# mLSTM value products of a two-layer hybrid block: one fp32 product replaced by three products of rounded parts, with the causal masks moved

## The chip, the core and the metric

One core of a Trainium2 chip runs the whole program. The metric is the device time of one execution in microseconds (us). PE is the matrix engine, DVE the vector engine, ACT the scalar engine, POOL the GpSimd engine and SP the queue that issues the weight loads.

## The reference

Two layers of a block over 512 tokens, 256 of context and 256 latent. Each layer projects the normed tokens to the inputs of three branches, merges them, and ends with an MLP. The change touches the mLSTM branch alone: four heads, keys and queries of width 128, values of width 256, each head scanned left to right and right to left.

```
def step(carry, inp):                       # one direction, one chunk
    d = where(tri, bcum[..., :, None] - bcum[..., None, :] + ic[..., None, :], -inf)
    m_t = maximum(inter, max(d, axis=-1))
    w_intra = exp(d - m_t[..., None])
    s_qk = einsum('bhtd,bhsd->bhts', qc, kc) * w_intra
    num = einsum('bhts,bhsv->bhtv', s_qk, vc) + w_inter[..., None] * einsum('bhtd,bhdv->bhtv', qc, c_mat)
    den = sum(s_qk, axis=-1) + w_inter * einsum('bhtd,bhd->bht', qc, n_vec)
    h_out = num / maximum(abs(den), exp(-m_t))[..., None]
...
h = h * rsqrt(mean(h * h, axis=-1) + EPS);  y = h.reshape(..., M_V) * gain * sigmoid(o_pre)
```

The kernel computes it without chunks: for each head and direction one weight matrix over all pairs of tokens (an exponential times the product of key and query), and the value product of it. Context tokens see only context; layer 1 needs the latent outputs alone.

## The kernel before

Tokens come in four tiles of 128 (`TT` = 4): tiles 0 and 1 are context, 2 and 3 latent. The order of all work is written out once, as a list of steps that `make_plan` builds (lines 184 to 443); each engine's program walks the same list and takes from each step what is its own. So an engine does its share strictly in the order of the steps, and waits at semaphores.

Large products (a "panel", 256 output columns by 8 k-tiles of 128) multiply in three products of parts. ACT rounds the weights of a panel to `wH` (L1526), DVE subtracts to get `wL` (L1989), both two panels ahead, and PE runs wH by hH, wL by hH and wH by hL (L1213, L1214, L1217). The parts have the type fp32r.

The steps of one mLSTM head h in layer 0 are, in order:

- `weigh`: PE makes the exponents, m0 and m1, one bank of PSUM for each direction (L1379), and the key-query products of key tiles 0 and 1 (L1386). ACT takes nine exponentials of them into `EP` (L1777, 2,560 columns; first all of one direction, then of the other; eight and 1,792 columns in layer 1).
- `part mo 0:2`: PE runs two of the eight k-tiles of the head's output-gate panel.
- `weigh_late`: PE makes the key-query products of key tiles 2 and 3 (L1394). They go to bank 0, which held m0, so this waits until the last exponential of that direction has read it. DVE then multiplies the exponentials by the products, in place (L2341), after all exponentials are there, and gives `P_ready`; POOL clears the wrong side of the diagonal blocks (L1944) after that.
- `norm_h` of head h-1: ACT squares the last tile of `hM` into `junk` for its sum (L1788), loads the table of the square root and takes it (L1792); DVE takes the reciprocal (L2376) and scales `hM` in place (L2378).
- `part mo 2:6`: four more k-tiles.
- `turn` of head h-1: PE transposes `hM` (L1420); ACT copies to `y_tmp` (L1799), DVE multiplies by the gate `sig_o` (L2387), ACT and POOL split the result (L1536, L1872).
- `value`: PE multiplies `EP` by the values `vaug` (L1410), which have a column of ones behind their 256, so that the denominator comes as column 257. The tiles come in the order 2, 3, 0, 1, each with two banks, one for each direction: 7, 7, 3 and 3 products. Tiles 0 and 1 use the banks of 2 and 3 again. For each tile DVE makes the divisors (L2357, L2361, L2364) and writes `hM` (L2365, L2368); ACT squares the first three tiles (L1788).
- `panel mo`: the last two k-tiles. ACT then splits the weights of a later panel (two L1526) and takes the gate's sigmoid `sig_o` by an exponential (L1592), with a table load ahead of it when the square root's table is in.

Layer 1 has the same steps with two tiles (14 value products a head), and `mo` is one whole panel between `norm_h` and `turn`. Head 0's `weigh` comes earlier there, ahead of the last values panel.

## Time and profile before

| | us |
|---|---|
| median of three runs (1830.58 to 1833.92) | 1832.34 |
| the profiled execution | 1831.94 |
| its span, first to last instruction | 1830.2 |
| PE busy | 1805.5 (99%) |
| DVE busy | 1052.3 (57%) |
| ACT busy | 724.8 (40%) |
| POOL busy | 176.7 (10%) |

The profiled execution has 1.74 us around its span. PE has next to no idle time, so what it is given to do sets the end, except at the few places where it waits. Matrix products are pipelined: a record's duration is longer than the distance to the next record, and what a stream of them costs is read from start to start. An fp32 product appears as two records. The mean granted clock of PE over the span is 0.998.

### The profile page before, as it was taken

Reading aid. Unit: us, or ns where it says so; the run is one execution under the profiler, and the core shown is the slowest. Engines: PE = TensorE matmul, PEld = TensorE weight load, DVE = VectorE, ACT = ScalarE, POOL = GpSimd, SP = SyncE. Lnnn points to the kernel's source line nnn. Section 1 sums busy time; section 2 is a strip of 40 time slices with the busy share of each in tenths; the row PEclk is TensorE's granted clock in tenths of the full one; section 3 lists DMA queues with packets and bytes.
Section 4 is the critical chain, followed back from the end, with each engine's and each line's share of the span. In section 5 each row is a group of like instructions: output and inputs, shape, how many; then the busy total and the mean of one; then the engine's idle time right before and its main releaser. Section 6 shows DMA issues by size and latency. Waiting matters only on the chain.

```text
span 1830.2 us, 24988 instructions
## 1 busy us (share of the span) xinstructions
PE 1805.5 (99%) x10187; PEld 1549.7 (85%) x10187; DVE 1052.3 (57%) x1538; ACT 724.8 (40%) x1011; POOL 176.7 (10%) x178
## 2 busy tenths in 40 slices
PE   7999999999999999999999999999999999999998
PEld 5887788888888888878888888788999999999997
DVE  5435635654557665467665645655557556566555
ACT  3424434544222222343232223444546544445444
POOL 2100101102110101220000000301110110120000
PEclk9999999999999999999999999999999999999999
DMA  9221122222543443535444536133142385565553
GB/s 312 92 93 47 35 84 67 70 70 70 173 148 98 158 165 106 183 106 198 138 138 141 190 96 195 54 130 94 53 133 93 122 253 185 183 225 178 191 184 116
DMA packets 214290, 245.55 MB, mean 134 GB/s; under 512 B 5836, under 2 KB 186400, under 8 KB 214176
## 3 DMA queue, kind: packets, MB, share of 16 engines
q1 hardware_dynamic: 213872, 243.85, 41.2%
q8 instruction: 81, 1.33, 0.3%
q14 instruction: 33, 0.27, 0.0%
q10 hardware_dynamic: 304, 0.10, 0.0%
HBM read 242.89 MB, written 1.05 MB: 133 GB/s over the span
## 4 chain that ended last, share of the span: by engine, by line
PE 92%; DVE 2%; ACT 2%; issue 1%; DMA 0%; POOL 0%; DVEq 0%; ACTq 0%; POOLq 0%
PE pp L1213 19%; PE pp L1217 19%; PE pp L1214 19%; PE pp L1221 4%; PE pp L1220 4%; PE pp L1222 4%; PE pc L1410 3%; PE pp L1144 2%; PE pp L1145 2%; PE pp L1146 2%; PE pc L1104 2%; PE pc L1103 2%; PE pc L1105 2%; PE pc L1482 1%; PE pc L1317 1%
## 5 line engine op out<-in xcount | busy, mean ns | idle before, releaser
L1989 DVE TENSOR_TENSOR wL<-raw,wH 128x1024 fp32r<-128x1024 f32 (+1 forms) x360 | 441.8, 1268 | 357.1 <-ACT wH L1526 355.0
L1213 PE MATMUL pp<-hH,wH 128*128 128x512 f32 (+1 forms) x1708 | 569.4, 344 | 0.6 <-ACT hH L1747 0.3
L1214 PE MATMUL pp<-hH,wL 128*128 128x512 f32 (+1 forms) x1708 | 560.2, 338 | 0.0
L1526 ACT ACTIVATE wH<-raw 128x1024 fp32r<-128x1024 f32 x360 | 361.1, 1051 | 454.8 <-DMA raw<-in_w_in 201.7
L1217 PE MATMUL pp<-hL,wH 128*128 128x512 f32 (+1 forms) x1708 | 439.3, 338 | 1.4 <-POOL hL L1920 0.8
L1213 PEld LDWEIGHTS pp<-hH,wH 128*128 128x128 f32 x1708 | 323.4, 189 | 43.3 <-issue 8.3
L1214 PEld LDWEIGHTS pp<-hH,wL 128*128 128x128 f32 x1708 | 323.6, 189 | 35.0 <-issue 1.0
L1217 PEld LDWEIGHTS pp<-hL,wH 128*128 128x128 f32 x1708 | 294.0, 189 | 37.6 <-POOL hL L1920 1.6
L1221 PE MATMUL pp<-yL,wH 128*128 128x512 f32 (+1 forms) x320 | 114.3, 357 | 0.0
L1220 PE MATMUL pp<-yH,wH 128*128 128x512 f32 (+1 forms) x320 | 114.3, 357 | 0.0
L1222 PE MATMUL pp<-yH,wL 128*128 128x512 f32 (+1 forms) x320 | 114.2, 357 | 0.0
L1213 PE MATMUL pp<-yH,wH 128*128 128x512 f32 (+1 forms) x320 | 113.6, 362 | 0.0
L1214 PE MATMUL pp<-yH,wL 128*128 128x512 f32 (+1 forms) x320 | 112.2, 357 | 0.0
L2188 DVE SCALAR_TENSOR_TENSOR acc<-pair_W,c_wide,acc 128x512 f32<-128x512 f32 x126 | 102.2, 848 | 3.8 <-DVE xT L2136 1.2
L1217 PE MATMUL pp<-yL,wH 128*128 128x512 f32 (+1 forms) x320 | 88.3, 357 | 0.0
L1536 ACT ACTIVATE yH<-y_tmp 128x1024 fp32r<-128x1024 f32 (+1 forms) x48 | 40.6, 846 | 85.9 <-DVE y_tmp L2120 41.5
L1213 PEld LDWEIGHTS pp<-yH,wH 128*128 128x128 f32 x320 | 60.3, 189 | 10.1 <-issue 1.6
L1222 PEld LDWEIGHTS pp<-yH,wL 128*128 128x128 f32 x320 | 60.4, 189 | 8.8
L1220 PEld LDWEIGHTS pp<-yH,wH 128*128 128x128 f32 x320 | 60.4, 189 | 8.8
L1221 PEld LDWEIGHTS pp<-yL,wH 128*128 128x128 f32 x320 | 60.4, 189 | 8.8
L1214 PEld LDWEIGHTS pp<-yH,wL 128*128 128x128 f32 x320 | 60.4, 189 | 8.4
L1217 PEld LDWEIGHTS pp<-yL,wH 128*128 128x128 f32 x320 | 56.9, 189 | 8.8
(286 smaller groups left out, 2343.2 us busy)
## 6 DMA issues: line engine op xcount, KB each, us to landing
raw<-in_w_in SPq DMA_DIRECT2D x83, 1024.0 KB, 5.2
raw<-in_w_up SPq DMA_DIRECT2D x32, 1024.0 KB, 5.4
raw<-in_w_down SPq DMA_DIRECT2D x32, 1024.0 KB, 5.1
pair_W<-in_w_ada SPq DMA_DIRECT2D x10, 2048.0 KB, 8.1
ada_Y<-in_w_ada SPq DMA_DIRECT2D x10, 1024.0 KB, 11.1
ada_H<-in_w_ada SPq DMA_DIRECT2D x8, 1024.0 KB, 12.2
raw<-in_w_proj_m SPq DMA_DIRECT2D x8, 1024.0 KB, 5.0
raw<-in_w_proj_a SPq DMA_DIRECT2D x8, 1024.0 KB, 5.2
```

The costliest lines, as they stand in the source:

```text
L1103: pe.matmul(banks[tt], yH[:, kt, ts_], wh[:, k_, :], start=first and k_ == 0, stop=False)
L1213: pe.matmul(dsts[b], wh[b], hi[:, kt, ts_], start=first, stop=False)
L1214: pe.matmul(dsts[b], wl[b], hi[:, kt, ts_], start=False, stop=False)
L1217: last = pe.matmul(dsts[b], wh[b], lo[:, kt, ts_], start=False, stop=end)
L1220: pe.matmul(dsts[b], wh[b], hi[:, kt, ts_], start=first, stop=False)
L1221: pe.matmul(dsts[b], wh[b], lo[:, kt, ts_], start=False, stop=False)
L1222: last = pe.matmul(dsts[b], wl[b], hi[:, kt, ts_], start=False, stop=end)
L1410: last = pe.matmul(b[:, 0:MV + 1], EP[:, d, off:off + P], vaug[:, s, h, :], start=i == 0, stop=i == len(terms) - 1)
L1526: act.activation(wH[:, p % HIGH, a:a + KH, :], raw[place_of[p]][:, a:a + KH, :], ACT.Copy).then_inc(wH_ready, 1)
L1536: act.activation(yH[:, kts, ts_], src, ACT.Copy).then_inc(yH_ready, 1)
L1989: dve.tensor_tensor(wL[place_of[p]][:, ks, :], raw[place_of[p]][:, ks, :], wH[:, p % HIGH, ks, :].bitcast(F32), ALU.subtract).then_inc(wL_ ...
L2188: i = dve.scalar_tensor_tensor(out=acc[:, v, :], in0=src[:, kt, :], scalar=c2[:, kt, v:v + 1], in1=acc[:, v, :], op0=ALU.mult, op1=ALU.add)
```

## The change

The value product of one pair of tiles was one fp32 product. Now ACT rounds the head's values to `mvH` (four tiles by 258 columns, 1,032) and the weighted exponentials to `EPH`; the rests `mvL` and `EPL` come by subtraction; PE runs EPH by mvH, EPH by mvL and EPL by mvH, 258 columns each, with two columns of ones instead of one. The rounding and the subtraction of the weights come in two halves (key tiles 0 and 1: 896 columns of each direction in layer 0, 512 in layer 1; key tiles 2 and 3: 384). ACT rounds all; DVE subtracts direction 0, POOL the values and direction 1. `EPL` has the place of `EP`, and `mvL` that of the head's values.

The exponentials come key tile by key tile, both directions together. POOL clears the diagonal blocks after the exponentials of a key tile and before DVE multiplies that tile. `P_ready` comes once for each half. The divisors take two DVE operations less for each tile. In layer 0 seven k-tiles of the output-gate panel stand ahead of the values and one behind them.

```diff
@@ make_plan
-                part("mo", l, h, 0, 2, 6)
+                part("mo", l, h, 0, 2, 7)
@@ PE, value
-                    pe.wait_ge(P_ready, n)
-                    pe.wait_ge(mask_ready, n)
...
+                    pe.wait_ge(mvL_ready, n)
+                    for d in range(2):
+                        pe.wait_ge(EPL_ready[d], 2 * n)
...
-                                last = pe.matmul(b[:, 0:MV + 1], EP[:, d, off:off + P], vaug[:, s, h, :],
-                                                 start=i == 0, stop=i == len(terms) - 1)
+                                hi, dst = EPH[:, d, off:off + P], b[:, 0:MV + 2]
+                                pe.matmul(dst, hi, mvH[:, s, :], start=i == 0, stop=False)
+                                pe.matmul(dst, hi, mvL[:, s, h, :], start=False, stop=False)
+                                last = pe.matmul(dst, EPL[:, d, off:off + P], mvH[:, s, :],
+                                                 start=False, stop=i == len(terms) - 1)
@@ ACT
+            def round_weights(l, h, half):
+                act.wait_ge(P_ready, 2 * (l * MH + h) + half + 1)
+                for d in range(2):
+                    cs = part_of(l, d, half)
+                    act.activation(EPH[:, d, cs], EP[:, d, cs], ACT.Copy).then_inc(EPH_ready, 1)
...
+                    act.activation(mvH[:, :, :], vaug[:, :, h, :], ACT.Copy).then_inc(mvH_ready, 1)
+                    round_weights(l, h, 0)
+                elif k == "weigh_late":
+                    round_weights(l, st["h"], 1)
@@ POOL
+            def weights_rest(l, h, half):
+                cs = part_of(l, 1, half)
+                pool.wait_ge(EPH_ready, 4 * (l * MH + h) + 2 * half + 2)
+                pool.tensor_tensor(EPL[:, 1, cs], EP[:, 1, cs], EPH[:, 1, cs].bitcast(F32), ALU.subtract
+                                   ).then_inc(EPL_ready[1], 1)
...
-                    pool.wait_ge(P_ready, l * MH + h + 1)
...
+                            pool.wait_ge(E_ready, e_count(l, h, s))
...
+                    pool.wait_ge(mvH_ready, l * MH + h + 1)
+                    pool.tensor_tensor(mvL[:, :, h, :], vaug[:, :, h, :], mvH[:, :, :].bitcast(F32),
+                                       ALU.subtract).then_inc(mvL_ready, 1)
+                    weights_rest(l, h, 0)
@@ DVE, weigh
-                    dve.wait_ge(E_ready, e_count(l, h))
...
+                        dve.wait_ge(E_ready, e_count(l, h, s))
...
+                        dve.wait_ge(mask_ready, mask_count(l, h, s))
...
+                    for half in range(2):
+                        cs = part_of(l, 0, half)
+                        dve.wait_ge(EPH_ready, 4 * (l * MH + h) + 2 * half + 1)
+                        dve.tensor_tensor(EPL[:, 0, cs], EP[:, 0, cs], EPH[:, 0, cs].bitcast(F32), ALU.subtract
+                                          ).then_inc(EPL_ready[0], 1)
@@ DVE, value
+                        link(dve.scalar_tensor_tensor(out=mstat[:, tt, 0:2], in0=both, scalar=-1.0, in1=least,
+                                                      op0=ALU.mult, op1=ALU.max))
+                        link(dve.tensor_tensor(mstat[:, tt, 2:4], both, mstat[:, tt, 0:2], ALU.max))
```

Three places show how instructions move. The first is ACT in layer 0, from the sigmoid of head 0 to the square root for head 0, which stands in head 1's steps. Before:

```order
L1592 ACTIVATE sig_o<-pp 128x1024
L1777 ACTIVATE EP<-pc,g_col 128x512
L1777 ACTIVATE EP<-pc,g_col 128x384
L1777 ACTIVATE EP<-pc,g_col 128x256
L1777 ACTIVATE EP<-pc,g_col 128x128 x2
L1777 ACTIVATE EP<-pc,g_col 128x256
L1777 ACTIVATE EP<-pc,g_col 128x512
L1777 ACTIVATE EP<-pc,g_col 128x128
L1777 ACTIVATE EP<-pc,g_col 128x256
L1788 ACTIVATE junk,mss<-hM 128x256
L1792 ACT_TABLE_LOAD
L1792 ACTIVATE mrs<-mss,small 128x4
```

And now:

```order
L1793 ACTIVATE EP<-pc,g_col 128x384
L1793 ACTIVATE EP<-pc,g_col 128x512
L1793 ACTIVATE EP<-pc,g_col 128x256
L1793 ACTIVATE EP<-pc,g_col 128x128 x2
L1793 ACTIVATE EP<-pc,g_col 128x256
L1799 ACTIVATE mvH<-vaug 128x1032
L1543 ACTIVATE EPH<-EP 128x896 x2
L1543 ACTIVATE EPH<-EP 128x384 x2
L1810 ACTIVATE junk,mss<-hM 128x256
L1814 ACT_TABLE_LOAD
L1814 ACTIVATE mrs<-mss,small 128x4
```

Five rounding copies stand between the last exponential and the square of the head before. The second place is DVE at the same head, from its last products to the scaling of head 0. Before:

```order
L2341 TENSOR_TENSOR EP<-EP,pc 128x128 x2
L2341 TENSOR_TENSOR EP<-EP,pc 128x256
L2376 RECIPROCAL mrs<-mrs 128x4
L2378 TENSOR_SCALAR hM<-hM,mrs 128x256 x4
L2387 SCALAR_TENSOR_TENSOR y_tmp<-sig_o,y_tmp 128x1024
```

And now:

```order
L2377 TENSOR_TENSOR EP<-EP,pc 128x128 x2
L2377 TENSOR_TENSOR EP<-EP,pc 128x256
L2390 TENSOR_TENSOR EPL<-EP,EPH 128x896
L2390 TENSOR_TENSOR EPL<-EP,EPH 128x384
L2416 RECIPROCAL mrs<-mrs 128x4
L2418 TENSOR_SCALAR hM<-hM,mrs 128x256 x4
L2427 SCALAR_TENSOR_TENSOR y_tmp<-sig_o,y_tmp 128x1024
```

Two subtractions stand ahead of the reciprocal. The third place is POOL, from the masks of head 2 of layer 0 on. Before:

```order
L1944 AFFINE_SELECT EP<-EP 128x128 x8
L1872 TENSOR_TENSOR yL<-y_tmp,yH 128x1024
L1944 AFFINE_SELECT EP<-EP 128x128 x8
L1872 TENSOR_TENSOR yL<-y_tmp,yH 128x1024 x2
L1952 TENSOR_TENSOR kL<-k_a,kH 128x1024
```

And now:

```order
L1973 AFFINE_SELECT EP<-EP 128x128 x8
L1976 TENSOR_TENSOR mvL<-vaug,mvH 128x4x258
L1899 TENSOR_TENSOR EPL<-EP,EPH 128x896
L1899 TENSOR_TENSOR EPL<-EP,EPH 128x384
L1894 TENSOR_TENSOR yL<-y_tmp,yH 128x1024
```

POOL gets three subtractions for each head, between its masks and the rest of the head before.

## Rows read from the trace of the kernel before

**Rows 1.** The page, busy time: us, share of the span, instructions.

```profile
PE 1805.5 (99%) x10187; PEld 1549.7 (85%) x10187; DVE 1052.3 (57%) x1538; ACT 724.8 (40%) x1011; POOL 176.7 (10%) x178
```

**Rows 2.** Instructions of line L1410: duration in ns (min/median/max), first and last start.

```profile
L1410 PE MATMUL pc<-vaug,EP x272: 378/380/484, 138.3 to 1312.6; 128*128 128x257 f32 x136
```

**Rows 3.** Timeline of PE, layer 0: start us, us, instruction, [idle before].

```profile
138.29 7.53 PE L1410 MATMUL pc<-vaug,EP 128*128 128x257 f32 x34
...
162.80 7.53 PE L1410 MATMUL pc<-vaug,EP 128*128 128x257 f32 x34
...
174.89 0.72 PE L1379 MATMUL pc<-M_parts,one_row 40*128 40x512 f32 x2
...
180.10 1.13 PE L1394 MATMUL pc<-qk 128*128 128x256 f32 x4
...
187.14 1.09 PE L1420 MATMUL pc<-con,hM 128*128 128x128 f32 x8 [0.42 <-DVE hM L2378]
188.07 7.53 PE L1410 MATMUL pc<-vaug,EP 128*128 128x257 f32 x34
```

**Rows 4.** Timeline of PE, layer 1: products of parts with 256 columns.

```profile
1315.43 0.28 PE L1182 MATMUL pp<-wL,hH 128*128 128x256 f32 x1
1315.55 0.28 PE L1183 MATMUL pp<-wH,hL 128*128 128x256 f32 x1
```

**Rows 5.** Timeline of ACT, layer 0, around the exponentials of head 2.

```profile
173.33 0.42 ACT L1788 ACTIVATE junk<-hM 128x256 f32<-128x256 f32 x1 [1.67 <-DVE hM L2368]
...
173.74 1.99 ACT L1526 ACTIVATE wH<-raw 128x1024 fp32r<-128x1024 f32 x2
175.75 1.28 ACT L1592 ACT_TABLE_LOAD   x1
...
178.27 3.61 ACT L1777 ACTIVATE EP<-pc,g_col 128x512 f32<-128x512 f32 x9 [0.19 <-ACT sig_o L1592]
181.71 0.47 ACT L1788 ACTIVATE junk<-hM 128x256 f32<-128x256 f32 x1
...
183.59 0.30 ACT L1792 ACTIVATE mrs<-mss,small 128x4 f32<-128x4 f32 x1
```

**Rows 6.** Timeline of DVE, the same stretch.

```profile
171.33 0.34 DVE L2357 TENSOR_SCALAR mstat<-pc,g_col 128x1 f32<-128x1 f32 x2 [0.22 <-DVE hM L2368]
...
181.96 3.34 DVE L2341 TENSOR_TENSOR EP<-EP,pc 128x512 f32<-128x512 f32 x9 [3.98 <-ACT EP L1777]
...
185.74 1.34 DVE L2378 TENSOR_SCALAR hM<-hM,mrs 128x256 f32<-128x256 f32 x4
```

**Rows 7.** Timeline of DVE and POOL where both run, at 185, 191 and 294.

```profile
185.52 2.21 POOL L1944 TENSOR_SCALAR_AFFINE_SELECT EP<-EP 128x128 f32<-128x128 f32 x8 [16.80 <-DVEq L2349]
...
191.62 2.36 POOL L1872 TENSOR_TENSOR yL<-y_tmp,yH 128x1024 fp32r<-128x1024 f32 x1 [3.90 <-ACT yH L1536]
...
192.86 0.48 DVE L2368 SCALAR_TENSOR_TENSOR hM<-pc,mstat,hM 128x256 f32<-128x256 f32 x1
...
294.08 2.97 DVE L2421 TENSOR_TENSOR q_a<-q_a,con 128x256 f32<-128x256 f32 x2
294.16 2.61 POOL L1952 TENSOR_TENSOR kL<-k_a,kH 128x1024 fp32r<-128x1024 f32 x1 [49.52 <-ACT kH L1822]
```

**Rows 8.** Instructions of L2421 and L2446 (DVE) over the whole program.

```profile
L2421 DVE TENSOR_TENSOR q_a<-q_a,con x16: 411/417/2640, 279.6 to 1386.5; 128x256 f32<-128x256 f32 x16
...
L2446 DVE TENSOR_SCALAR pr<-pr,ars x48: 340/482/1534, 312.3 to 1443.9; 128x512 f32<-128x512 f32 x32, 128x256 f32<-128x256 f32 x16
```

**Rows 9.** Timelines of PE and ACT, layer 1, heads 2 and 3.

```profile
1291.73 6.23 PE L1410 MATMUL pc<-vaug,EP 128*128 128x257 f32 x28
1297.89 0.50 PE L1379 MATMUL pc<-M_parts,one_row 40*128 40x256 f32 x2
...
1306.73 6.23 PE L1410 MATMUL pc<-vaug,EP 128*128 128x257 f32 x28
...
1298.51 2.82 ACT L1777 ACTIVATE EP<-pc,g_col 128x256 f32<-128x256 f32 x8 [0.97 <-PE pc L1379]
```

More of the change, by code:

```diff
@@ L792, in trunk @@
         mask_ready = sem("mask_ready")
+        EPH_ready = sem("EPH_ready")
+        EPL_ready = [sem(f"EPL_ready{d}") for d in range(2)]
+        mvH_ready = sem("mvH_ready")
+        mvL_ready = sem("mvL_ready")
         hraw_ready = sem("h_out_ready")
@@ L1772, in _ @@
                         act.wait_ge(full[bk], un + 1)
[L1773 to L1780 removed]
+                    ms = [bank(act, u[f"m{d}"]) for d in range(2)]
+                    for s in range(TT):
+                        for d, a, e, off in rows_of(l, s):
+                            last = act.activation(EP[:, d, off:off + e - a], ms[d][:, m_cols(l, d, a, e)], ACT.Exp, scale=-1.0,
+                                                  bias=g_col[:, d, s, d * MH + h:d * MH + h + 1])
+                            frees = (s, a) == (TT - 1, packed(l, d)[s][-1][0]) and (l < DEPTH - 1 or d)
+                            last.then_inc(free[u[f"m{d}"][0]] if frees else E_ready, 1)
+                    act.wait_ge(mv_ready, MH * l + h // 2 * 2 + 2)
+                    act.wait_ge(vones, l + 1)
+                    act.activation(mvH[:, :, :], vaug[:, :, h, :], ACT.Copy).then_inc(mvH_ready, 1)
+                    round_weights(l, h, 0)
+                elif k == "weigh_late":
+                    round_weights(l, st["h"], 1)
                 elif k in ("value", "norm_h"):
@@ L2331, in _ @@
                     whole = l < DEPTH - 1
-                    for d in range(2):
-                        dve.wait_ge(free[u[f"m{d}"][0]], u[f"m{d}"][1] + 1)
-                    dve.wait_ge(E_ready, e_count(l, h))
                     for s in range(TT):
@@ L2337, in _ @@
                         b = bank(dve, us)
-                        todo = [(d, a, e, off) for d in range(2) for a, e, off in packed(l, d)[s]]
+                        dve.wait_ge(E_ready, e_count(l, h, s))
+                        if s == TT - 1:
+                            for d in range(2):
+                                dve.wait_ge(free[u[f"m{d}"][0]], u[f"m{d}"][1] + 1)
+                        dve.wait_ge(mask_ready, mask_count(l, h, s))
+                        todo = rows_of(l, s)
                         for n, (d, a, e, off) in enumerate(todo):
@@ L2502, in _, with rows_of, part_of, e_count @@
                         scaled(1)
-def e_count(l, h):
-    per = [sum(len(r) for d in range(2) for r in packed(q, d)) - (2 if q < DEPTH - 1 else 1) for q in range(DEPTH)]
-    return sum(per[q] * MH for q in range(l)) + per[l] * (h + 1)
+def rows_of(l, s):
+    return [(d, a, e, off) for d in range(2) for a, e, off in packed(l, d)[s]]
+def part_of(l, d, half):
+    row = [r for s in (2 * half, 2 * half + 1) for r in packed(l, d)[s]]
+    return slice(row[0][2], row[-1][2] + row[-1][1] - row[-1][0])
+def e_count(l, h, s):
+    def upto(q, s):
+        return sum(len(rows_of(q, t)) for t in range(s + 1)) - (0 if s < TT - 1 else 2 if q < DEPTH - 1 else 1)
+    return sum(upto(q, TT - 1) * MH for q in range(l)) + upto(l, TT - 1) * h + upto(l, s)
+def mask_count(l, h, s):
+    def upto(q, s):
+        return sum(a <= t * P < e for t in range(s + 1) for d, a, e, off in rows_of(q, t))
+    return sum(upto(q, TT - 1) * MH for q in range(l)) + upto(l, TT - 1) * h + upto(l, s)
 def h_count(l, h, tt):
```

77 lines of the change are left out of this document (35 added, 42 removed).

## The prediction, made before the changed kernel ran

> **What bounds the kernel now.** I read the busy times first [rows 1]: PE is busy for 1805.5 of 1830.2 us, so work that leaves PE shortens the run, as long as nothing else is late. Then the value products [rows 2]: 272 records, that is 136 fp32 products. Last the timelines of PE, ACT and DVE around one head, to see how far ahead of PE the others run [rows 3, 5, 6]. They are hardly ahead. PE already waits 0.42 us at the transposes of a head (187.14) for the scaling of hM on DVE. So from head 1 on, a loop through ACT and DVE sets the pace of layer 0, and PE just fits in it. What the change puts on that loop counts in full.
>
> I write V for the start of a head's value products, W for PE's exponents of the next head, X for ACT's first exponential. All durations are of the profiled execution.
>
> **What PE saves.** 34 records of L1410 take 7.53 us; without the last one's tail (0.38 less about 0.22) they lie 0.217 us apart, so an fp32 product costs 0.433 us [rows 2, 3]. A product of parts with 256 columns follows its neighbour by 0.120 us [rows 4]. 258 columns have no row. The bounds are 0.12 and the 0.217 of a 257-column pass. I take 0.121, since 256 columns of the same type are nearest and two columns more are 1%. Three of them are 0.363, so 0.070 us is saved for each of 136, 9.6 us in all if nothing is late.
>
> The Trainium skill, in "TensorE: Matmul & The Clock Gate", section "Back-to-back issue gap", gives the lone gap as the columns over 2.4 GHz plus 2.5 ns, which is 0.110 us for 258 columns. By that estimate 14 us would leave PE. The 0.120 of the row decides.
>
> **From V to X in layer 0.** Before, this took 15.47 us (162.80 to 178.27) [rows 3, 5]: the third tile's square comes at 10.53 (173.33), and from there to X two weight copies, a table load, the sigmoid and a write wait take 4.94. Now tiles 2 and 3 have 21 products each: full at 2.8 and 5.34 us (21 and 42 times 0.121, and 0.26 for the tail and the hand-over). A pair of divisor operations takes 0.34 us and stands twice in a tile [rows 6]; with one operation on both columns in place of a pair I take 0.13 off each, so a tile's DVE work falls from 2.18 us (171.33 to the square at 173.33, and 0.18 more until the next tile) to 1.92. The ends are 0 and 0.34 off each pair; the loop moves by at most 0.4 us. Tile 3 runs 5.34 to 7.26, tile 0's hM is written at 9.0, the square starts at 9.04, X is V + 13.95. That is 1.5 us won. Head 1 has no table load of 1.28 us ahead of its sigmoid: X = V + 12.5.
>
> **From X to the next V in layer 0.** Before, 9.8 us [rows 3, 5, 6]: exponentials (3.45 by starts), square and root, end at 5.6; DVE multiplies from 3.7 to 7.0, scales hM from 7.5 to 8.8; transposes 0.93. The step that now fails to hide is on ACT. A copy of 1,024 columns costs 0.96 us of ACT (two in 1.99) [rows 5]: mvH 0.97, EPH 0.86 and 0.86, then 0.43 and 0.43. They stand ahead of the square. P_ready for the first half comes at about 4.4 (the first tile's exponentials, masks of 0.28 us each [rows 7], and DVE with 3.34 us for all nine multiplications [rows 6]), just as mvH ends. So the copies run 4.46 to 7.04, and the root, 2.18 us after them, ends at 9.2. DVE alone would then have hM scaled at 11.0.
>
> **POOL and DVE.** Here the rows say more. DVE's L2421 takes 0.417 us in the median, but 2.64 us once [rows 8]; that is the one at 294.08, beside POOL's kL of 2.61 us at 294.16 [rows 7]. A scaling from SBUF to SBUF (L2446) is held in the same way, 1.53 us at worst [rows 8]. An operation with PSUM and one SBUF tensor (L2368, 192.86) keeps its 0.48 beside POOL [rows 7]. So DVE's EPL and its scaling of hM are held while POOL subtracts, and DVE's multiplications are not. POOL takes 2.36 us for 1,024 columns [rows 7]: mvL 2.4 (4.6 to 7.0), EPL 2.1 and 1.0. In turns: DVE EPL to 7.9, POOL to 10.0, DVE EPL to 10.4, POOL to 11.4. The first scaling is held to 11.4, the four end at 12.3. PE turns at X + 12.35 instead of 8.87, V is X + 13.2 instead of 9.8. EPL of direction 1 (11.4) is not last for heads 1 to 3; for head 0 it is ready 11.5 us after 127.3 (its exponentials), 138.8, and seven k-tiles bring PE there at 138.29 + 1.37 = 139.66: no stall.
>
> The Trainium skill has this rule in "GPSIMD Engine Reference", section "8. Key points": GpSimd shares its SBUF interfaces with VectorE and contends with VectorE instructions that have two SBUF inputs or run in a two-port mode. By that rule the rows above are the normal case; without it the sum would be that of the second case below. The trace agrees with 2.64 against 0.417 us.
>
> Two other waits grow but lie inside. Bank 0 is free only after the eighth exponential, X + 3.3, while W + 5.2 (174.89 to 180.10) [rows 3] is X + 0.4 for heads 2 and 3: PE stalls 2.9 us there, then needs 7.7 us to the transposes and is ready at X + 11.0, ahead of hM. The weight copies come two panels early, and a panel here spans a period of some 25 us; masks earlier cost POOL the same eight operations; the DMA order is unchanged.
>
> **Sum, layer 0.** Moved k-tile ahead of head 0: +1.37. V to V, head 1: 12.5 + 13.2 = 25.7 against 24.51 (138.29 to 162.80): +1.2. Heads 2 and 3: 13.95 + 13.2 = 27.2 against 25.27: +1.9 each. After the last V: 7.77 of products with their wait for bank 2, and one k-tile, 9.14, against 12.09 (162.80 to 174.89) [rows 3]: -2.95. Together +3.4 us.
>
> **Sum, layer 1.** Period before 15.0 (1291.73 to 1306.73), X 0.61 after W (1297.89 to 1298.51) [rows 9]. Now 42 products take 5.1. From X: exponentials 2.66, mvH to 3.6, EPH to 5.6, root 7.7. POOL mvL 3.8 to 6.2, DVE EPL to 6.75, POOL to 8.0, DVE to 8.4, POOL to 9.4, two scalings to 9.75; transposes 0.45; V = X + 10.25. Period 10.25 + 5.1 + 0.65 = 16.0: +1.0 three times, and the last head's products -1.0: +2.0 us. Head 0 has a panel between.
>
> Both layers: +5.4. The profiled execution gives 1831.94 + 5.4 = 1837.3, the median 1837.7: **I forecast 1837.5**. Six loops with some 0.4 us of doubt each make it 1835 to 1840. A difference of 0.2% (3.7 us) is about the least that can be told from none.
>
> **The rivals.**
> - POOL and DVE do not hold each other here (each gets in between the other's reads). For it speaks that the four scalings at 185.74 take their 1.34 us beside POOL's masks [rows 6, 7]; against it, 2.64 us at 294.08. Then the scaling ends at X + 11.0 in layer 0: V to V 24.4, 25.85 and 25.85, sum -0.5 us. In layer 1 it ends at X + 8.8, the period is 15.0 to 15.5, the sum -1.0 to +0.5. Both layers -0.7: 1831.5. Chance 0.25.
> - The cover is enough, PE stays the bound, and the run is faster. This is one mechanism: ACT's five copies and the square fit while PE runs the seven k-tiles. It decides if X comes within 1 us of W; rows 3 and 5 have X 3.4 us after W (174.89, 178.27), and earlier W makes it 4.8. Then 9.6 us are won and some stalls with them: 1822. Chance 0.12.
> - PE's clock falls. Its mean is 0.998, so after the start it was at 2.4 GHz through waits of at most 0.4 us in this part. With waits of 2 to 3 us at six heads it may go down to 1.2 GHz. A stretch at that level loses half its length; with 2 us lost at four heads it is 1845. Chance 0.08.
> - The products of 258 columns cost 0.217 as a 257-column pass does: PE then has +0.22 for each of 136, 30 us, of which the loop hides little. 1862. Chance 0.02, since the type is that of rows 4.
>
> The forecast's own case has 0.53.
>
> **How the numbers follow.** Of the forecast's case 0.05 lies below 1836. Faster 0.12, same 0.30 (0.25 and 0.05), slower 0.58 (0.48, 0.08 and 0.02). The range leaves out the case of 1822, the 1862, and the upper part of the clock's: 1829 to 1844.
>
> **What would show it.** In the new profile: products of 258 columns 0.121 us apart; POOL's three subtractions in turns with DVE's EPL, one of which takes over 1.5 us; the transposes 12.3 us after the first exponential in layer 0 and 9.8 in layer 1; PE idle about 1 us before each of them and near 3 us before the late key-query products of heads 2 and 3; no wait at head 0. It would be wrong if the transposes stood within 11 us of X, if the values waited for EPL and not for hM, or if granted clock fell below 1.

## The result: slower by 9.8 us, inside the range of the prediction

| | kernel before | changed kernel |
|---|---|---|
| median of 5 runs | 1832.01 us | 1841.74 us |
| lowest and highest | 1830.58, 1833.92 | 1838.99, 1845.69 |
| profiled execution, its span | 1831.94, 1830.2 | 1841.74, 1840.0 |

The ratio is 1.0054, with a 95% interval of 1.0039 to 1.0068. Forecast was 1837.5 us, range 1829 to 1844. The spans differ by 9.8 us. Single executions far above the others of their kernel (from 2,228 us up) count in no ratio and in no range below.

The page of the changed kernel, busy time (us, share of the span, instructions), against [rows 1]:

```profile
PE 1801.4 (98%) x10323; PEld 1553.0 (84%) x10323; DVE 1076.4 (58%) x1506; ACT 750.0 (41%) x1051; POOL 221.1 (12%) x202
```

PE is busy 4.1 us less than before and the span is 9.8 us longer, so PE idles 13.9 us more. The list of PE's waits from 126 to 1345 us says where (us in total, times, longest):

```profile
PE pc L1430 <- DVE hM L2418: 6.9, 4, 2.0
PE pc L1402 <- ACT EP L1793: 4.8, 3, 2.2
...
PE pc L1394 <- DVE hM L2405: 1.3, 3, 0.7
```

L1430 are the transposes of a head (L1420 before), L1402 the late key-query products (L1394 before), L1394 the first ones. Before, the transposes waited 0.8 us in all and the key-query products did not wait.

Timeline of PE in layer 0, values (L1418 is the first of each three), next head's exponents, key-query products and transposes, against [rows 3]:

```profile
139.65 0.28 PE L1418 MATMUL pc<-mvH,EPH 128*128 128x258 f32 x1
148.84 0.73 PE L1387 MATMUL pc<-M_parts,one_row 40*128 40x512 f32 x2
150.26 1.95 PE L1394 MATMUL pc<-qk 128*128 128x512 f32 x4 [0.70 <-DVE hM L2405]
...
164.14 1.09 PE L1430 MATMUL pc<-con,hM 128*128 128x128 f32 x8 [0.84 <-DVE hM L2418]
...
182.11 1.13 PE L1402 MATMUL pc<-qk 128*128 128x256 f32 x4 [2.20 <-ACT EP L1793]
...
191.53 1.03 PE L1430 MATMUL pc<-con,hM 128*128 128x128 f32 x8
192.32 0.36 PE L1418 MATMUL pc<-mvH,EPH 128*128 128x258 f32 x1
```

Head 0's values start at 139.65, 1.36 us later than before, and wait for nothing. The transposes of heads 2 and 3 (191.53 and 218.86) show no wait: there PE itself comes last. Timelines of ACT, DVE and POOL around the same head, against [rows 5] and [rows 6]:

```profile
178.81 3.61 ACT L1793 ACTIVATE EP<-pc,g_col 128x512 f32<-128x512 f32 x9 [0.26 <-ACT sig_o L1609]
182.25 1.12 ACT L1799 ACTIVATE mvH<-vaug 128x1032 fp32r<-128x1032 f32 x1
183.22 2.65 ACT L1543 ACTIVATE EPH<-EP 128x896 fp32r<-128x896 f32 x4
...
187.59 0.30 ACT L1814 ACTIVATE mrs<-mss,small 128x4 f32<-128x4 f32 x1
...
184.70 4.31 DVE L2390 TENSOR_TENSOR EPL<-EP,EPH 128x896 fp32r<-128x896 f32 x2 [0.17 <-DVE EP L2377]
188.93 0.17 DVE L2416 RECIPROCAL mrs<-mrs 128x4 f32<-128x4 f32 x1
189.13 1.69 DVE L2418 TENSOR_SCALAR hM<-hM,mrs 128x256 f32<-128x256 f32 x4
...
183.45 2.21 POOL L1976 TENSOR_TENSOR mvL<-vaug,mvH 128x1032 fp32r<-128x1032 f32 x1 [0.34 <-ACT mvH L1799]
185.62 4.26 POOL L1899 TENSOR_TENSOR EPL<-EP,EPH 128x896 fp32r<-128x896 f32 x2
```

This is the predicted chain: X at 178.81, root done at X + 9.1, DVE's two EPL stretched to 4.3 us beside POOL, hM scaled at X + 12.0. But PE turns only at X + 12.7. Why, the granted clock shows. Windows of the changed kernel: start and end, length, busy time of PE, PEld, DVE, ACT and POOL, then PE's granted clock, DMA share and GB/s. The first two follow the waits for bank 0 in layer 0, the other three hold the values of heads 1 to 3 in layer 1:

```profile
183.00:187.00 4.00, 4.00 (x13) 3.10 (x12) 3.59 (x7) 3.98 (x8) 3.65 (x3) 0.57 0.01 2
209.40:214.00 4.60, 4.56 (x14) 3.65 (x14) 3.84 (x9) 4.58 (x9) 4.08 (x6) 0.64 0.01 2
1280.20:1286.10 5.90, 5.90 (x48) 5.64 (x47) 4.32 (x11) 3.52 (x8) 1.30 (x1) 1.00 0.37 129
1295.60:1302.80 7.20, 7.19 (x47) 7.06 (x47) 4.37 (x8) 3.87 (x8) 1.29 (x1) 0.76 0.37 130
1312.90:1320.00 7.10, 7.09 (x47) 7.09 (x48) 4.37 (x8) 3.89 (x8) 1.29 (x1) 0.76 0.39 134
```

Between 184 and 186 us the granted clock is 0.50, the 1.2 GHz level. In layer 1 all three windows follow a wait of 2.0 us at the transposes. After the first the clock stays at 1.00 and the 42 products take 5.19 us (1280.21 to 1285.40). After the second and third it falls, and they take 6.70 and 6.53 us.

To place the 9.8 us I took the same ACT instruction in both profiles and subtracted its start:

| up to | difference so far | added in the stretch |
|---|---|---|
| end of the heads of layer 0 (vH) | +3.1 | +3.1 |
| end of layer 0's attention | +3.6 | +0.5 |
| 820 us | +2.0 | -1.6 |
| first output panel of layer 1 (sig_o) | +2.3 | +0.3 |
| end of the heads of layer 1 (vH) | +7.2 | +4.9 |
| end of layer 1's attention | +9.7 | +2.5 |
| end | +9.8 | +0.1 |

The -1.6 is the kernel before: its granted clock was 0.91 from 790 to 810 us, where it runs small products between two norms, and that of the changed kernel 1.00. The +2.5 is a wait that nobody had in view, for ACT's copy of an attention output; the last three experiments deal with it.

### The profile page after: what moved, and what is told of

Its sections match the earlier page's. It is cut to its first block, busy times and chain, and to the rows that moved or that the text cites. A ratio compares the mean times of both kernels' runs of the same rounds, so it can differ in the third digit from the quotient of the medians.

```text
span 1840.0 us, 25346 instructions
## 1 busy us (share of the span) xinstructions
PE 1801.4 (98%) x10323; PEld 1553.0 (84%) x10323; DVE 1076.4 (58%) x1506; ACT 750.0 (41%) x1051; POOL 221.1 (12%) x202
## 3 DMA queue, kind: packets, MB, share of 16 engines
q8 instruction: 82, 1.34, 0.3%
## 4 chain that ended last, share of the span: by engine, by line
PE 90%; DVE 3%; ACT 3%; DMA 1%; issue 1%; POOL 0%; DVEq 0%; ACTq 0%; POOLq 0%
PE pp L1221 19%; PE pp L1225 18%; PE pp L1222 18%; PE pp L1229 4%; PE pp L1228 4%; PE pp L1230 4%; PE pp L1152 2%; PE pp L1153 2%; PE pp L1154 2%; PE pc L1112 2%; PE pc L1111 2%; PE pc L1113 2%; DVE EPL L2390 1%; PE pc L1418 1%; PE pc L1419 1%
## 6 DMA issues: line engine op xcount, KB each, us to landing
ada_H<-in_w_ada SPq DMA_DIRECT2D x8, 1024.0 KB, 11.9
```

## Experiments

My theory was that the loop through ACT and DVE sets the pace of the heads: V to X, then exponentials, copies, norm, scaling of hM (held by POOL), transposes, V. The new trace added that PE's clock falls behind some of the waits that the loop makes. Ratios are to the kernel before on the same chip, whose median was 1830.7 to 1831.0 us there; the changed kernel's own is 1.0054.

**Six k-tiles ahead again.**

```
-                part("mo", l, h, 0, 2, 7)
+                part("mo", l, h, 0, 2, 6)
```

> The changed kernel with six k-tiles of the next output panel ahead of a head's values and two behind, as before, instead of seven and one. My theory (the scaling of hM on DVE, held by POOL's subtractions, sets the turn; PE's granted clock of 0.5 after the bank-0 wait makes PE some 0.7 us later than that in heads 2 and 3): head 0's values start 0.85 us earlier, heads 2 and 3 gain 0.6 us each because PE is in time again, and the last head has one k-tile more behind its values, +1.37 us. Sum -0.7 us against the changed kernel, some 1841 us, within the noise. Rival (the seventh k-tile is cover that PE needs): PE waits 1.37 us more at three turns, +3 to +4 us, 1845 us. Rival (the moved k-tile is what cost the time): -3 us or more, 1838 us.

Measured 1841.4 us, ratio 1.0057 (1.0045 to 1.0069). The moved k-tile made no difference, as expected. PE's waits moved from bank 0 (2.4 us instead of 4.8) to the transposes (12.6 instead of 6.9). Its profiled execution has four falls of the clock, two of them outside the heads (at 804 and 1168 us).

**Four k-tiles ahead of the late key-query products.**

```
-                part("mo", l, h, 0, 0, 2)
+                part("mo", l, h, 0, 0, 4)
-                part("mo", l, h, 0, 2, 7)
+                part("mo", l, h, 0, 4, 7)
```

> The changed kernel with four k-tiles, not two, between PE's exponents and its late key-query products in layer 0 (then the other three; still seven ahead of the values). PE then has 2.75 us of products to run while bank 0 is not yet free. My theory (the 2.2 us wait there brings PE's granted clock down to 0.5 for some 3.5 us and so PE comes to the turn 0.7 us behind hM): the wait falls below 0.5 us, the granted clock stays at 1.00 up to the turn, the turn of heads 2 and 3 follows hM within 0.1 us, -1 to -2 us in layer 0, about 1840 us. The last transposes then wait 1.5 to 3 us for hM instead, which may cost the clock afterwards. Rival (the late products come too late for DVE's multiplications, now 0.6 us after they are wanted): turn 0.5 us later, +1 to +2 us. Rival (the clock costs nothing here): no change, and the turn stays 12.7 us behind the first exponential.

Measured 1844.13 us, ratio 1.0076 (1.0062 to 1.0089): a miss. The interval overlaps that of the changed kernel, and the profiled span is 2.2 us longer, of which 2.0 are there by the end of the heads of layer 0. The wait for bank 0 is gone and the scaling of hM still ends 12.0 us behind X. But now PE waits 1.9 us (head 1) and twice 3.2 us right before the transposes, and behind the first two of these waits the clock falls, on the values. PE's timeline, and the windows of the values of heads 1 and 2:

```profile
164.50 1.61 PE L1430 MATMUL pc<-con,hM 128*128 128x128 f32 x8 [1.89 <-DVE hM L2418]
...
192.75 1.97 PE L1430 MATMUL pc<-con,hM 128*128 128x128 f32 x8 [3.20 <-DVE hM L2418]
```

```profile
165.00:169.00 4.00, 4.00 (x23) 4.00 (x22) 1.23 (x1) 2.22 (x3) 0.00 (x0) 0.58 0.00 0
192.00:196.00 4.00, 3.25 (x17) 3.25 (x18) 1.18 (x4) 1.38 (x2) 0.00 (x0) 0.57 0.00 0
```

In the changed kernel the slow stretch fell on k-tiles, which have slack of some 1 us until hM is there. Here it falls on the values, which the loop waits for. An idle time was moved, not removed, to where its after-effect costs more.

**Most of POOL's subtractions left out.**

```
-                    pool.tensor_tensor(mvL[:, :, h, :], vaug[:, :, h, :], ...
+                    pool.tensor_tensor(mvL[:, :, h, 0:2], vaug[:, :, h, 0:2], ...
+                cs = slice(cs.start, cs.start + 8)
-                                pe.matmul(dst, hi, mvL[:, s, h, :], start=False, stop=False)
-                                last = pe.matmul(dst, EPL[:, d, off:off + P], mvH[:, s, :],
+                                pe.matmul(dst, hi, mvH[:, s, :], start=False, stop=False)
+                                last = pe.matmul(dst, (EPH if d else EPL)[:, d, off:off + P], mvH[:, s, :],
```

> Leaves out most of POOL's subtractions: the low part of the values is made for two columns of each k-tile, and EPL of direction 1 for eight columns of each half; PE's products of direction 1 and of the low part read the high parts in their place, so PE runs the same number and shape of products on wrong data. Everything else stands. My theory (POOL's subtractions hold DVE's): DVE's two EPL of a head in layer 0 take 1.5 us instead of 3.5 to 4.3, its four scalings 1.34 instead of 1.69, hM is done 10.7 us behind the first exponential instead of 12.0. The turn of head 1 is 1.35 us earlier; those of heads 2 and 3 stay with PE, which is late by its clock, at 12.7. In layer 1 the turn comes 1 us earlier in each of three heads, and with waits of 1 us instead of 2 the granted clock falls less, up to 1.5 us more each. Sum -4 to -9 us, 1833 to 1838 us. Rival (ACT's copies alone set it, POOL holds nobody): EPL on DVE still takes its 3.5 us or more, no change, 1841 us.

Measured 1836.58 us, ratio 1.0032 (1.0020 to 1.0044), some 4 us less than the changed kernel. Groups of DVE by line and form (busy us, mean ns), of the changed kernel:

```profile
L2390 DVE TENSOR_TENSOR EPL<-EP,EPH 128x384 fp32r<-128x384 f32 x8 | 16.5, 2063 | 0.0
L2418 DVE TENSOR_SCALAR hM<-hM,mrs 128x256 f32<-128x256 f32 x24 | 10.3, 484 | 0.3
L2390 DVE TENSOR_TENSOR EPL<-EP,EPH 128x896 fp32r<-128x896 f32 x4 | 6.5, 1619 | 0.7 <-DVE EP L2377 0.5 <-ACT EPH L1543 0.2
```

and of this one:

```profile
L2419 DVE TENSOR_SCALAR hM<-hM,mrs 128x256 f32<-128x256 f32 x24 | 7.0, 350 | 0.3
L2391 DVE TENSOR_TENSOR EPL<-EP,EPH 128x384 fp32r<-128x384 f32 x8 | 4.5, 560 | 0.5
L2391 DVE TENSOR_TENSOR EPL<-EP,EPH 128x896 fp32r<-128x896 f32 x4 | 4.4, 1093 | 0.7 <-DVE EP L2378 0.3 <-ACT EPH L1543 0.3
```

The same DVE instructions take 560 ns instead of 2063, 1093 instead of 1619, and 350 instead of 484 when POOL does not subtract beside them. So POOL's subtractions hold DVE's. It goes both ways: POOL's own EPL of 896 columns takes 2983 ns in the mean in the changed kernel, its yL of 1,024 columns 2499. The Trainium skill, "GPSIMD Engine Reference", section "8. Key points", has the rule: GpSimd contends with VectorE instructions that have two SBUF inputs or run in a two-port mode. By that rule EPL is held as the first kind and the scaling as the second; the trace agrees, with 2063 against 560 ns and 484 against 350.

The terms of DVE came out as expected (two EPL in 1.57 us, the scalings in 1.14, hM at X + 10.5), the total at the low end: of heads 2 and 3 of layer 0 nothing was won, since PE came last there. By the profiles the heads of layer 0 gain 1.1 us and those of layer 1 gain 4.1. Of these 4.1 some 2.8 are the clock, which did not fall behind the three waits that are left there, of 1.0 us each; so the hold itself is worth about 1.1 us in layer 0 and 1.3 in layer 1.

**Four moves together.**

```
+            step("vsplit", l, h=h + 1)      # behind value(h); POOL: mvH, then mvL
+                step("rounds", l, h=h)      # EPH and EPL, behind norm_h
-                part("mo", l, h, 0, 0, 2)
+                part("mo", l, h, 0, 0, 4)
-                for d in range(2):
+                for d in (1, 0):            # ACT's EPH
```

> The changed kernel with four moves together: POOL makes the high part of a head's values as well as the low one, and makes both ahead of that head's exponentials, while it is idle; ACT and DVE take the norm of the head before (square, root, scaling of hM) ahead of the rounding of the weights and EPL; ACT rounds direction 1, POOL's, first; four k-tiles stand ahead of the late key-query products in layer 0. My theory (the loop first exponential, copies, norm, scaling, turn, values is what costs, not the products): in layer 0 the turn comes 8 us behind the first exponential instead of 12.1 to 12.7, the values wait for EPL at 10.5 to 11, so a head's period is 23 to 24.6 us instead of 25.3 to 27.3; in layer 1 values start 9 us behind the first exponential instead of 10.2, period 14.4 instead of 15.8 to 17.3, with few waits over 1 us and a granted clock near 1. Sum -14 to -17 us against the changed kernel, 1825 to 1828 us, and 4 to 7 us below the kernel before. Rival (POOL's four subtractions and copy are too slow, a cast of 1,032 columns over 3 us, or EPL gates at 12 us): no better than the kernel before, 1832 us. Rival (the products of parts themselves cost more than they save): above 1840 us.

Measured 1832.27 us, ratio 1.0004 (0.9995 to 1.0013): 9 us won back, level with the kernel before, but 4 to 7 us short of what I expected. The profile shows a part of the miss: direction 1 first lets POOL start earlier (184.75), just when DVE scales hM. Timeline of DVE:

```profile
184.44 3.76 DVE L2434 TENSOR_SCALAR hM<-hM,mrs 128x256 f32<-128x256 f32 x4
```

3.76 us instead of 1.34 [rows 6]. A head's period in layer 0 was 25.4 us (164.37 to 189.77).

**The parts of it.** First the values' split early on POOL alone:

> One part of the four-move kernel alone: POOL makes both parts of a head's values, ahead of that head's exponentials; ACT's copy mvH is gone from the loop, POOL's mvL no longer stands between masks and EPL. My theory (what follows the first exponential X on ACT, and what POOL holds on DVE, sets the turn): in layer 0 ACT gains nothing, because its copies wait for DVE's first half at X + 4.4 anyway, but POOL is done at X + 9 and DVE's scaling runs in 1.34 us: hM at X + 10.7 instead of 12.0. Head 1 gains 1.3 us, heads 2 and 3 stay with PE at X + 12.7. In layer 1 ACT is 1 us earlier and the scaling not held: turn at X + 8 instead of 9.5, three times, and the granted clock falls less. Sum -5 to -9 us against the changed kernel (which is 9.8 us over the kernel before): 1832 to 1836 us. Rival (it is the order norm behind rounding that counts, not mvH and mvL): under 2 us, 1839 us.

Measured 1839.36 us, ratio 1.0040 (1.0027 to 1.0053), by 4 runs: about 2.5 us won, between the two cases and nearer to the rival. Then with the norm ahead of the rounding:

> Two parts of the four-move kernel: POOL makes both parts of the values early, and the norm of the head before (square, root, scaling) goes ahead of the rounding. Direction 0 is still rounded first, and two k-tiles stand ahead of the late key-query products. My theory: without direction 1 first POOL starts its EPL 0.9 us later, so DVE's four scalings take 1.3 to 1.5 us instead of the 3.76 of the four-move kernel, and hM is done 7.2 us behind X; but PE comes to the turn only at X + 11 to 12.7 after its wait for bank 0 of 2.2 us and the fall of its clock, so layer 0 ends where the split alone puts it or 1 us earlier. Layer 1 has period 14.7 as the four-move kernel has. 1831 to 1834 us. Rival (EPL sets the values' start): values wait for EPL over 1 us in layer 0.

Measured 1833.5 us, ratio 1.0013 (1.0004 to 1.0022), as the theory said. DVE's four scalings take 1.14 us again, and in layer 0 the values wait for EPL nowhere; PE still waits 2.2 us for bank 0:

```profile
184.22 1.14 DVE L2434 TENSOR_SCALAR hM<-hM,mrs 128x256 f32<-128x256 f32 x4
```

On top of the split, the order norm ahead of rounding is worth the larger share, 5 us; alone it was not run.

**PE's waits in layer 1 filled.**

```
+                    if l and h < MH - 1:
+                        b = claim(u[0])
+                        for _ in range(12):
+                            pe.transpose(b[:, 0:P], ident, ident)
                     pe.wait_ge(hn_ready, l * MH + h + 1)
```

> The changed kernel with twelve transposes of the identity into the bank that the head's transposes use, before PE waits for hM, in layer 1, heads 0 to 2. They compute nothing and take some 1.6 us of the 2.0 us in which PE is idle there. Theory (the idle 2.0 us bring PE's granted clock to half, so the values of 5.1 us take 1.4 us longer): the transposes start where they did, 9.5 us behind X, the granted clock stays above 0.98, and each head of layer 1 gains about 1.4 us: -3 to -4.5 us, 1836 to 1837.5 us. Rival (the clock has another cause, or the loss sits elsewhere): period and total unchanged, 1840.5 us.

Measured 1836.33 us, ratio 1.0032 (1.0020 to 1.0044). The work of the loop is the same, and PE does work that nobody needs. Its timeline around head 2, and the windows of the values of heads 1 to 3:

```profile
1291.83 1.47 PE L1430 MATMUL pc<-con 128*128 128x128 f32 x12
1294.01 0.66 PE L1435 MATMUL pc<-con,hM 128*128 128x128 f32 x4 [0.72 <-DVE hM L2423]
```

```profile
1278.00:1284.00 6.00, 5.82 (x47) 5.70 (x48) 4.46 (x10) 4.05 (x8) 1.29 (x1) 1.00 0.46 159
1294.00:1300.00 6.00, 5.99 (x48) 5.75 (x48) 4.46 (x10) 3.90 (x8) 1.29 (x1) 1.00 0.44 154
1310.00:1316.00 6.00, 6.00 (x52) 6.00 (x52) 4.40 (x10) 3.72 (x7) 1.30 (x1) 1.00 0.40 140
```

The clock is 1.00 in all three, the period is 15.8 us twice, and layer 1's heads add 1.9 us instead of 4.9. That is one execution, the fastest of seven, and its clock fell nowhere, not even behind the waits of 2.2 us in layer 0 that nobody filled; the mean clocks of the seven run from 0.999 down to 0.994. This kernel also has 36 records more on PE, and its wait in layer 1's attention was gone as well, so the gain needed a control (below).

**Copies early.** To the split and the norm this adds one move on ACT, in layer 0 alone, and three k-tiles ahead of the late products:

```
+            if more:
+                step("copies", l, c=h)      # ACT: the panel's two weight copies
             step("value", l, h=h)
-                part("mo", l, h, 0, 0, 2)
+                part("mo", l, h, 0, 0, 3)
-                part("mo", l, h, 0, 2, 7)
+                part("mo", l, h, 0, 3, 7)
```

> Split early and norm first as in the kernel before this one, three k-tiles ahead of the late key-query products in layer 0 instead of two, and in layer 0 ACT's two weight copies of the output panels (1.99 us) go from behind the third tile's square to ahead of the first, into idle time. Theory (in layer 0 the way from V to X is as much part of the loop as the way from X to V): X comes 11.8 us behind V instead of 13.8, bank 0 is free in time, and the period of a head falls to what PE needs, 22.9 to 23.3 us (25.4 in the four-move kernel), with the values' waits for EPL under 0.5 us. Layer 1 has period 14.7. Sum 5 to 7 us below the four-move kernel: 1825 to 1827 us, 4 to 6 us below the kernel before. Rival (the sigmoid waits for PE's last k-tile and the table load, or POOL's chain cast, mvL, masks, EPL is the next bound): under 2 us gained on the four-move kernel, about 1831 us.

Measured 1827.73 us, ratio 0.9978 (0.9969 to 0.9987): the fastest median of the study, 3.2 us below the kernel before by the medians and 4.0 by the ratio. The period in layer 0 fell to 24.1 us (187.35 to 211.48 from values to values), not to 23. X does come 11.9 us behind V, and then EPL is last. DVE's timeline:

```profile
181.93 3.02 DVE L2438 TENSOR_SCALAR hM<-hM,mrs 128x256 f32<-128x256 f32 x4
184.87 2.38 DVE L2410 TENSOR_TENSOR EPL<-EP,EPH 128x896 fp32r<-128x896 f32 x2
```

Both are held by POOL (1.14 and 1.57 us in the kernel without most of its subtractions), so the hold is the next bound. The median is 0.7 us above the range that I expected.

**The move of the copies without products of parts.**

> The kernel before with one move of the best variant alone: in layer 0 ACT's two weight copies of the output panels go from behind the third tile's square to ahead of the first. The value products stay fp32. Theory (in the kernel before PE has 24.9 to 25.3 us of work in a head's period, so the loop through ACT cannot be much shorter than it is, and only products of parts make room for what the moves free): PE's waits of 0.2 to 0.4 us per head go, -0.5 to -1 us, 1830 to 1830.5 us. Rival (the moves and not the products are what makes the best variant fast): -2 us or more, below 1829 us.

Measured 1829.06 us, ratio 0.9986 (0.9978 to 0.9995). That is -1.9 us by the medians and -2.6 by the ratio, at the rival's edge (-2 and more) and not where my theory had it (-0.5 to -1). So more than half of the best variant's gain is this move, which has nothing to do with the change. What the products of parts add, with their loop repaired, is some 1.4 us by the medians, and the intervals of the two kernels overlap: that they pay at all is not clear of the noise. By the profiles the end of layer 0's heads is 1.6 us earlier than before in this kernel and 5.0 us in the best variant.

**PE's code moved, in three kernels.**

```
                     filled(pe.transpose(claim(u["par2"])[:, 0:16], par_rows[2][0:16, :], ident[0:16, 0:16]), u["par2"])
+                    for _ in range(36):      # 14 in the kernel before
+                        pe.transpose(pp[:, 1, 1, 0:16], par_rows[2][0:16, :], ident[0:16, 0:16])
```

The wait is PE's, at the transposes of the last probabilities of layer 1, in the timeline of the changed kernel:

```profile
1456.36 0.66 PE L1492 MATMUL pc<-con,pr 128*128 128x128 f32 x4 [1.70 <-ACT q_a L1857]
```

ACT is late because it copies a weight panel first, and that panel landed late. DMA of the changed kernel from 1440 to 1460 us (KB each, us from issue to landing), and queue q8, which brings code, from 1449 to 1450 (packets, MB, share of 16 engines):

```profile
raw<-in_w_proj_a SPq DMA_DIRECT2D x1, 1024.0 KB, 6.9
```

```profile
q8 instruction: 1, 0.02, 12.1%
```

In the kernel with filled waits the panel took 5.0 us, and the packet came ahead of it, alone, in half the time (5.8%, one engine for 0.93 us):

```profile
raw<-in_w_proj_a SPq DMA_DIRECT2D x1, 1024.0 KB, 5.0
```

> The variant with copies early, with 36 small transposes (16 columns each) in PE's program at its start, where PE waits 3.2 us for x. They compute nothing and only move PE's code. Theory (a packet of PE's code on queue q8, 16 to 18 us from the next, falls into the transfer of a weight panel near 1436 us, holds one of the 16 DMA engines for 2 us, and that panel, copied by ACT ahead of the attention's output, makes PE wait 1.5 us): with the code moved by 36 records the packet lies ahead of that transfer, PE's wait of 1.5 us at the next probability transposes is gone, and the span is 1.0 to 1.7 us shorter: 1826 to 1826.7 us. Rival (the transfer is late for another reason, or another packet meets another transfer): no change, 1827.7 us.

> The changed kernel with the same 36 small transposes at the start: as many records as the kernel that fills PE's waits in layer 1 has, but none in the waits. It tells that kernel's two effects apart. Theory (both are real): the wait of 1.7 us in layer 1's attention is gone, the rest stands: -1.5 to -2 us, 1838.5 to 1839.2 us; what remains to the 1836.3 us of the filled kernel, 2 to 3 us, is the clock in layer 1. Rival (all of the filled kernel's gain was the place of the code): 1836.3 us. Rival (all was the clock): 1840.6 us.

> The kernel before with 14 small transposes at the start. Its code packet comes near 1443 us, at the tail of the panel's transfer (1440 to 1444 us), and costs nothing; 14 records of some 0.12 us each bring it 1.7 us forward, into the transfer, where it lies in the changed kernel. Theory: the packet then takes about twice its 0.93 us on its engine, the transfer takes 6 us or more instead of 5.2, and layer 1's attention has a wait for ACT's q_a copy of 1 to 1.7 us: +1 to +1.7 us, 1832 to 1832.7 us. Rival (a chance of single executions, not of the code's place): no change, 1831 us.

The 36 transposes were meant to fall into a wait and cost nothing. They cost something: in both kernels that have them PE later waits 1.7 us for an ada_H panel, and in the twelve others at most 0.7 to 0.8. Changed kernel, then the changed kernel with the code moved:

```profile
PE pc L1325 <- DMA ada_H<-in_w_ada: 0.7, 1, 0.7
PE pc L1327 <- DMA ada_H<-in_w_ada: 1.7, 1, 1.7
```

ACT's copy qk of layer 0 then starts at 71.66 us instead of 70.28, and in the best variant at 71.74 instead of 70.19. So both kernels carry 1.4 to 1.5 us from their start, which none of the expectations had. Why the panel lands later is open.

Best variant with the code moved: 1828.07 us, ratio 0.9987 (0.9978 to 0.9996). Its packet lies ahead of the transfer (5.1 us), the wait of 1.5 us is gone and its profiled span of 1824.5 us is the shortest of all. But its median is no better than that of the best variant: the start takes back what the wait gave. Its times also spread more, from 1826.2 at a mean clock of 0.998 to 1832.3 at 0.994, those of the best variant from 1827.0 to 1830.1. The profile bears the theory out as far as the wait goes, and the median does not.

Changed kernel with the code moved: 1838.66 us, ratio 1.0047 (1.0034 to 1.0059). The number is the one the theory gave, in part by luck, since the theory did not have the start. The wait is gone, and layer 1's attention adds nothing. Its heads show the clock at work once more, behind three waits of 2.0 us each:

```profile
1280.00:1286.00 6.00, 6.00 (x48) 5.76 (x48) 4.46 (x10) 3.90 (x8) 1.29 (x1) 1.00 0.44 152
1296.00:1302.00 6.00, 6.00 (x39) 6.00 (x39) 3.93 (x8) 3.18 (x5) 1.29 (x1) 0.73 0.42 146
1313.00:1319.00 6.00, 5.86 (x49) 5.86 (x50) 4.47 (x10) 4.02 (x8) 1.30 (x1) 1.00 0.46 156
```

As a control for the filled kernel it is flawed by its start. By the profiles the filled kernel is 3.35 us shorter: 1.6 by the start of the heads (1.4 of it the added transposes), 0.55 in layer 0 (one fall of the clock fewer) and 1.2 in layer 1 (one fall fewer). By the medians it is 2.3 us shorter, and without the transposes 0.9, which is within the noise; at the same mean clock, 0.997, its executions take 1835.95 and 1836.33 us and that of the control 1838.04. So these two runs do not show that filling the waits saves time by the clock.

Kernel before with the code moved by 14 records: 1832.01 us, ratio 1.0009 (0.9999 to 1.0018). Inconclusive: the packet went further than I meant, to 1438 us, ahead of the transfer and not into it. The transfer took 5.0 us and the wait was 0.4. That a packet can be pushed into a transfer was not shown; that the wait is gone with the packet out of it was, three times. The other profiles agree. In the eight kernels where the packet starts in the transfer, over 1.3 us from its end, the panel lands after 6.1 to 7.0 us and PE's longest wait for q_a is 0.8 to 1.8 us. In the six where it comes ahead of the transfer or in its last 1.3 us, these are 4.9 to 5.3 us and at most 0.5 us.

## Why the prediction was right, and where it was not

- **The products.** They follow each other by 0.12 us with 258 columns (1318.42, 1318.54, 1318.66), as taken from [rows 4], and the last rival, 0.217, is out.
- **V to X.** Forecast 12.5 for head 1 and 13.95 for heads 2 and 3 (less the table load of 1.28, 13.95 gives 12.67 and not 12.5). Measured 12.4 (139.65 to 152.06) and 13.8 (164.99 to 178.81). The divisor pair is now two operations of 0.16 us, a little shorter than assumed.
- **X to the transposes, layer 0.** Forecast 12.35, with hM scaled at 12.3. Head 1 has 12.1 (152.06 to 164.14), and hM is scaled at X + 12.0. Copies, root and hold all came within 0.4 us of their term; leaving POOL's part out confirmed the hold, so the rival of 1831.5 us is out. The faster rival needed X within 1 us of W; X came 3.2 us behind it at head 1 (148.84 to 152.06). For heads 2 and 3 the step failed that PE would be ready at X + 11.0. After the bank-0 wait of 2.2 us it ran at half clock, and came at X + 12.7. In the profile of the filled kernel, whose layer 0 is the same and whose clock did not fall, PE came in time and waited 0.8 us for hM there.
- **Bank 0.** Wait forecast 2.9, measured 2.2; PE came to it later than I had it, because the first key-query products waited 0.3 to 0.7 us for bank 2, a wait I did not have.
- **Sum of layer 0.** Forecast +3.4, measured +3.1. That the two agree is luck: the half clock is 1.2 of the 3.1 (the periods of heads 2 and 3 are 27.3 us, and 26.8 and 26.7 in the filled kernel, where the clock did not fall), so the loop alone gave +1.9, little over half of the forecast. Without the clock heads 1 to 3 each came some 0.4 to 0.6 us below their forecast period, because every term from V to X and from X to V was a little too large, and head 3 was set against 25.27 us where it took 25.54 before (188.07 to 213.61).
- **Layer 1.** Forecast X to V 10.25, period 16.0, sum +2.0. Measured 9.9 (1270.27 to 1280.21) and 15.85 for the first period (1264.36 to 1280.21). PE's idle time before the transposes was 2.0 us each time, and the signs had said about 1. The later values took 1.5 and 1.3 us longer by the clock. Sum +4.9; without these 2.8 us it is +2.1. So here the mechanism and its size held, and the term that was missing is the clock.
- **The clock rival.** I gave it 0.08 and priced it at 1845. Its condition came about: the text said that it would be wrong if the granted clock fell below 1, and it did, in four stretches. It cost 4.1 us in this execution (1.2 in layer 0 and 2.85 in layer 1), not 7.5. The step that failed is the chance, not the mechanism. In the profiles of the eight kernels that have waits of 1.9 to 3.2 us in the heads, 16 of 30 such waits have a fall behind them: about half for each wait, and so much more than 0.08 for six of them.
- **Not foreseen.** +2.5 us in layer 1's attention, from code packets that met weight transfers. And -1.6 us, because the kernel before had lost time to its clock in the profiled execution from which I summed.

So the forecast of 1837.5 was 4 us low, and the 1835 to 1840 us around it did not hold either. Missing were the clock (+4.1) and the packets (+2.5); against them stand the loop of layer 0, which was forecast 1.5 us too dear, and the 1.6 us that the kernel before had lost in its own profile. The median of the changed kernel holds the clock too: its five times run with the mean clock, from 1838.99 us at 0.998 to 1845.69 us at 0.994.

## What to carry to other kernels

Where a loop through other engines sets the pace, shortening the bound engine's work turns into its waits; look first for what can leave the loop (here the norm ahead of the rounding, and copies and splits into idle time), since four such moves gave 9 us back. That brought the changed kernel level with the one before; whether the products of parts pay beyond that is within the noise. Price every new wait on TensorE twice: once for itself, and once for the slower stretch that may follow it, by which work lies there. Sum against a profile only after looking at its own granted clock, and try the helpful move without the change as well: more than half of the best variant's gain was there. Compare a control with its parent from the first microsecond on: the transposes that moved the code cost 1.4 us where they were thought free.

## What the runs showed of the hardware

- A wait of 2.0 us on PE brought the granted clock down in some cases and not in others: of six such waits in layer 1 (changed kernel, and with its code moved) three were followed by 0.73 to 0.76 in the window of the values and three by 1.00. In the heads of all profiles it is 16 of 30 waits of 1.9 to 3.2 us, and none of 19 of 1.0 to 1.5 us. The clock fell at other places too: 0.91 from 790 to 810 us in the kernel before, 0.83 from 790 to 800 and from 1157 to 1167 us in the best variant. One execution does not tell what a wait costs.
- With twelve transposes that compute nothing, 1.47 us in a wait of 2.0, the clock was 1.00 behind all three waits of the one execution that was profiled. That they kept it there is not shown.
- DVE operations from SBUF to SBUF beside a POOL subtraction: 2063 ns instead of 560 (EPL of 384 columns, mean), scalings of 256 columns 484 instead of 350 in the mean, up to 3.76 us for four. POOL's subtraction of 896 columns took 2983 ns beside DVE's. DVE operations that read PSUM kept their 0.48 us.
- A packet of PE's code (0.02 MB, one DMA engine for 0.93 us when alone, 1.9 us when it shares) came every 9 to 21 us in layer 1's attention. A transfer of 1 MB with such a packet in it landed after 6.1 to 7.0 us instead of 4.9 to 5.3; that the one engine with the packet trails the other 15 would explain it, and is not shown. The Trainium skill, "Runtime: NRT & Kernel Launch", section "Instruction fetch mechanics", says that an engine's code comes in blocks of 16 KiB, 256 instructions, over a DMA queue of its own. The trace agrees: 0.02 MB, and 128 products with their weight loads at 0.12 us each are 15.4 us. It adds that this fetch is hidden. No wait of PE is put down to it here, but the weights beside it landed later.
